# The weight load beside the index queries' rope: issued behind the eight row swaps instead of in front of them

## The reference

```python
    u = rms_norm(x, norm_g) * (1 + scale[:, None]) + shift[:, None]     # "the third norm"
    z = u @ w_in
    (aq, ak, av, ag, iq, ik, iw, bq, bk, bv, bg, cq, ck, cv, cg, ma, mb, mc) = jnp.split(z, SPLIT_OFFSETS, axis=-1)
    ...
    ya = dsa_attention(rope(aq), rope(ak), av, rope(iq), rope(ik), iw)   # iq, ik, iw choose the keys

def apply_rope(x, cos, sin):
    x1, x2 = jnp.split(x.astype(jnp.float32), 2, axis=-1)
    return jnp.concatenate([x1 * c - x2 * s, x1 * s + x2 * c], axis=-1).astype(x.dtype)
```

## Time and profile before

| | us |
|---|---|
| median of 3 runs | 2800.11 |
| the runs | 2791.91, 2800.11, 2801.91 |
| the profiled execution | 2794.37 |
| its span | 2792.6 |
| PE busy | 2681.3 (96%) |
| DVE busy | 1816.1 (65%) |
| ACT busy | 1152.6 (41%) |
| DMA from issue to landing, 1 MB weight load, median | 5.3 |
| DMA from issue to landing, 64 KB swap, median | 2.2 |

### The profile page before, as it was taken

The page is one execution under the profiler, slowest core; times in us unless marked ns, Lnnn a source line. Parts: engine busy times, 40 slices in busy tenths (PEclk is TensorE's granted clock), DMA queues, the critical chain, the costliest instruction groups (busy, mean ns, idle before and its releaser), DMA issues.

```text
span 2792.6 us, 36953 instructions
## 1 busy us (share of the span) xinstructions
PE 2681.3 (96%) x14886; PEld 2154.3 (77%) x14886; DVE 1816.1 (65%) x2968; ACT 1152.6 (41%) x1900; POOL 693.0 (25%) x514
## 2 busy tenths in 40 slices
PE   6999899999999998999999999998999999999997
PEld 5877578888878676888887878776787788777776
DVE  7789668867577775877557768744546548544534
ACT  3243544323242454433224464344434455444432
POOL 0000047988700004356540032000100122000100
PEclk9999999999999998999999999999999999999999
DMA  8453034554432112344432535231223222322312
GB/s 273 122 144 104 29 121 151 166 166 159 147 119 57 59 59 83 121 143 150 139 123 85 163 94 159 85 106 33 91 64 106 85 73 80 91 76 72 96 61 78
DMA packets 281114, 302.59 MB, mean 108 GB/s; under 512 B 9968, under 2 KB 263024, under 8 KB 280944
## 3 DMA queue, kind: packets, MB, share of 16 engines
q1 hardware_dynamic: 267568, 250.21, 28.8%
q0 software_dynamic: 13088, 49.55, 5.4%
q10 hardware_dynamic: 288, 0.47, 0.1%
HBM read 289.97 MB, written 2.10 MB: 105 GB/s over the span
## 4 chain that ended last, share of the span: by engine, by line
PE 86%; DVE 7%; ACT 4%; DMA 1%; issue 1%; SPq 0%; POOL 0%; DVEq 0%; ACTq 0%
PE ps L568 84%; PE ps L776 2%; DVE wl L1410 1%; DVE hl L1416 1%; DVE adaacc L1416 1%; DMA raw<-in_w_in 1%; ACT wh L934 0%; DVE recat L1708 0%; ACT recat L934 0%; ACT hh L934 0%; DMA stage<-in_w_ada 0%; DVE rawt L1416 0%; DMA t1s<-rawt 0%; ACT att_p L934 0%; DVE ca L1416 0%
## 5 line engine op out<-in xcount | busy, mean ns | idle before, releaser
L568 PE MATMUL ps<-hh,wh 128*128 128x512 f32 x2208 | 891.8, 404 | 24.1 <-DVE wl L1410 10.2
L568 PE MATMUL ps<-hh,wl 128*128 128x512 f32 x2208 | 866.8, 393 | 0.0
L568 PE MATMUL ps<-hl,wh 128*128 128x512 f32 x2208 | 865.5, 392 | 0.0
L1410 DVE TENSOR_TENSOR wl<-raw,wh 128x2048 fp32r<-128x2048 f32 (+3 forms) x234 | 500.9, 2149 | 167.7 <-ACT wh L934 167.5
L568 PEld LDWEIGHTS ps<-hh,wh 128*128 128x128 f32 x2208 | 416.5, 189 | 140.8 <-issue 40.4
L568 PEld LDWEIGHTS ps<-hh,wl 128*128 128x128 f32 x2208 | 416.4, 189 | 92.4
L568 PEld LDWEIGHTS ps<-hl,wh 128*128 128x128 f32 x2208 | 417.3, 189 | 80.2
L934 ACT ACTIVATE wh<-raw 128x2048 fp32r<-128x2048 f32 (+3 forms) x234 | 370.0, 1591 | 205.8 <-PE ps L568 191.4
L568 PE MATMUL ps<-fh,wh 128*128 128x512 f32 x432 | 171.6, 397 | 0.0
L568 PE MATMUL ps<-fh,wl 128*128 128x512 f32 x432 | 168.3, 390 | 0.0
L568 PE MATMUL ps<-fl,wh 128*128 128x512 f32 x432 | 168.2, 389 | 0.0
(11 more groups left out here) (298 smaller groups left out, 4136.5 us busy)
## 6 DMA issues: line engine op xcount, KB each, us to landing
raw<-in_w_in SPq DMA_DIRECT2D x75, 1024.0 KB, 5.3
raw<-in_w_up SPq DMA_DIRECT2D x46, 1024.0 KB, 5.1
strewn<-in_w_ada POOLq DMA_DIRECT2D x80, 512.0 KB, 4.1
raw<-in_w_ada SPq DMA_DIRECT2D x24, 1024.0 KB, 5.3
raw<-in_w_in SPq DMA_DIRECT2D x44, 512.0 KB, 5.1
raw<-in_w_out SPq DMA_DIRECT2D x16, 1024.0 KB, 5.1
raw<-in_w_down SPq DMA_DIRECT2D x16, 1024.0 KB, 5.2
stage<-in_w_ada SPq DMA_DIRECT2D x8, 1024.0 KB, 11.6
```

The lines of the kernel that those rows point to most:

```text
L568: return e.matmul(o, a, b, start=start, stop=stop, skip_group_check=True)
L1410: return e.tensor_tensor(o, a, b, op)
```

## The change

Of the splits in the list, the one that stands right in front of the unit `em` of a third norm (`split cq0`) no longer issues loads. The loads that it freed are issued at `rope iq1` instead, after its four swaps. All engines but SP have the same instructions in the same order.

```diff
-    for kind, *rest_ in X.order:
+    for n, (kind, *rest_) in enumerate(X.order):
         if kind == "rope":
             rope(*rest_[:3])
         elif kind in ("split", "ada", "adap"):
             free.add(rest_[-1])
+        if kind == "split" and X.order[n + 1][:1] == ("em",) and X.order[n + 1][1][0] == "m3":
+            continue
+        if kind in ("split", "ada", "adap") or kind == "rope" and rest_[1:3] == ["iq", 1]:
             while loads and loads[0][1]["raw_before"] in free:
                 load(*loads.pop(0))
```

## The result

| | before | changed |
|---|---|---|
| median | 2798.22 us, 20 runs | 2791.29 us, 20 runs |
| lowest and highest | 2787.97, 2806.32 | 2780.86, 2799.48 |
| the profiled execution's span | 2792.6 | 2795.5 |

The ratio is 0.9976, 95% interval 0.9966 to 0.9985: 6.7 us less, with an interval of 4.2 to 9.5. The forecast was 8.45 us less and 2791.7.

A forecast was written before the change was run, and what follows sets the result against it. PE, busy 96% of the span, was taken as the bound, leaving its idle time and low-clock stretches to gain. Layer 0's 4.3 us plus layer 1's 4.15 made 8.45 us (0.30%), from 2800.11 to 2791.7, range 2783 to 2800.

The forecast's parts named there:

- Landing with the load: Third norm, both layers: a swap issued behind the weight load waits for it; without it, landing was taken as 2.0 us.
- Layer 1, 4.15 forecast: PE sets the end: `cq1` starts 2.55 us earlier and regains 1.6 us of clock, together 4.15 us.
- The rival in which the clock does not come back: Layer 1, `cq1`: low clock stays, so the layer gives 2.55 us and the whole 6.9, 2793.2; chance 0.10.
- Layer 0, 4.3 forecast: DVE sets the end: its `wl` of `ck0` comes earlier and the gain goes on; 4.3 us taken.
- DVE's restart: Layer 0: DVE waits for `iq1` until 1523.6, then two steps of 0.7 us end at 1525.0 instead of 1529.63.
- the 4.6 of the undisturbed case: Layer 0: DVE's `rest iq1` ends 4.6 us earlier with 2.0 us landings, before other items cost some tenths.
- the 0.3 that I had: Layer 0: DVE loses 0.3 us beside POOL's `ik` product; if the row's 1.0 us returned whole, the layer gives 3.6.
- The late load: Layer 0: `ck0`'s load, now last, has cover of 0.3 us at 5.9 us landing, 1.0 us at the median landing.
- The slower rival: The late load decides: layer 0 loses from a landing of x = 10.8 us on; 15 us gives 2805; chance 0.04.
- The swaps slow of themselves: Both layers: eight swaps in a row stay slow and only start 1.07 us earlier; 2798.0, chance 0.05.
- More comes back: Layer 0: low-clock stretches behind both idle times go too, up to twice 1.6 us more; 2788.5, chance 0.05.
- The waits forecast for the profile: ACT waits for `iq0` 2.5 us (layer 0), 3.5 (layer 1), for `ck0`'s load some 5; PE idles 2 to 3 before `ck0`.

The follow-up runs named there:

- e3: Changed kernel with the load behind the four swaps of `iq0` only, ahead of those of `iq1`; ratio to before 0.9972, layer 0 distance 30.94 us.
- e6: Kernel before, old order, the moved load bringing only one eighth of its chunk; distances 30.03 us (layer 0) and 15.29 us (layer 1), no ratio.
- e5: Against the changed kernel, the load is issued at its old time from ACT's DMA queue, the swaps staying on SP's; ratio to before 0.9992.
- e1: Kernel before with the load moved behind the eight swaps in layer 0 only; ratio to before 0.9971, layer 0 distance 29.42 us.
- e11: Changed kernel with forty fulfilled waits on DVE at the start of the last feed-forward products; layer 0 distance 29.63 us, no ratio.
- e4: Changed kernel with the load behind all ten swaps, those of `ik` too; ratio to before 0.9963, layer 0 distance 30.56 us.
- e8: Changed kernel with forty fulfilled waits on SP ahead of the loads of the last feed-forward products; ratio to before 0.9965, layer 0 distance 29.18 us.
- e10: Changed kernel with forty fulfilled waits on PE behind the second tile of the last feed-forward products; layer 0 distance 28.96 us, no ratio.

## Why the prediction was right

*Forecast and sum.* The mechanism held at every step that carries it, and the sum of 8.45 us stands against 2.9 + 4.3 = 7.2 by the traces and 6.7 (4.2 to 9.5) by the runs. That the median of 2791.29 lies only 0.4 us from the forecast of 2791.7 is luck: the forecast started from a median of 3 runs, 2800.11, which 20 runs put 1.9 us lower, and the gain was forecast some 1.5 us too large. The two errors cancel. And 14 us, which I took as the least that can be told from no change, was too coarse: 20 runs of each kernel gave an interval of 4.2 to 9.5 us.

*Landing with the load* is shown by e3 (swaps behind the load are late, those ahead are not) and e6 (few bytes, swaps of 2.0 us in layer 1, and in layer 0 but for those beside the packet), and e5 adds what the rows before could not say, that the queue is not the reason.

*Layer 1, 4.15 forecast, 4.3 measured.* All eight swaps landed in 1.9 to 2.0 us, where 2.0 was taken, ACT's wait came out at 3.48 where 3.5 was forecast, and `cq1` starts with no idle time and runs at 1.00. The rival in which the clock does not come back had its chance in eight kernels that moved the load here behind the swaps of `iq0`; the distance was 15.1 and the granted clock over the tile 1.00 in each. The Trainium skill (TensorE: Matmul & The Clock Gate, Part 1) has the monitor's window run freely, by which rule this could change from run to run. The start of the kernel, 0.86 against 0.95 in the first 70 us, agrees with that; at this tile no trace showed it.

*Layer 0, 4.3 forecast, 3.6 in the profiled pair, 2.9 on average.* The term that was mis-sized is DVE's restart, which came later than summed up. I had `iq1` landed 7.15 us behind the mark and two steps of 0.7 us after it. DVE's timeline of the changed kernel:

```profile
1532.96 0.69 DVE L1410 TENSOR_TENSOR t1s<-t1s,cst 128x512 f32<-128x512 f32 x1 [4.39 <-DMA t1s<-rawt]
1533.69 0.69 DVE L1410 TENSOR_TENSOR iq<-iq,t1s 128x512 f32<-128x512 f32 x1
1535.00 1.17 DVE L1410 TENSOR_TENSOR t1s<-t1s,cst 128x512 f32<-128x512 f32 x1 [0.62 <-DMA t1s<-rawt]
1536.20 0.69 DVE L1410 TENSOR_TENSOR iq<-iq,t1s 128x512 f32<-128x512 f32 x1
...
1542.05 2.28 DVE L1410 TENSOR_TENSOR wl<-raw,wh 128x2048 fp32r<-128x2048 f32 x1
```

`iq1` was there at 7.76, 0.6 late: SP's chain has one swap that took 1.25 us to issue instead of 0.6 (1.88 in e1, where layer 0 came out 0.7 us worse). And its first step took 1.17 us, beside POOL's product of `ik`, 1.29 us from 1534.33 on. Together they take 1.1 us off the 4.6 of the undisturbed case, of which I had kept 4.3. The price was 0.5 us, not the 0.3 that I had nor the 1.0 of the row before. The Trainium skill (SBUF — State Buffer, "Who interferes with whom") has the instruction issued second wait until the first is over. By that rule DVE would wait until 1535.62 and end at 1536.31; the trace has 1536.17 and agrees within 0.14 us.

*The late load.* It landed in 6.4 us, not 5.9, `wh` was done at 1541.94, and DVE came to `wl` at 1542.05. The cover of 0.3 us that I gave it was 0.1, and in e11, where the load took 6.9 us, DVE waited 0.27 us for `wh`. The slower rival never came near: its x of 10.8 us stands against 6.4, and with the load 2.3 us later still, in e4, the layer keeps 1.8 us.

*The swaps slow of themselves* is out: the eight of layer 1 landed in 1.9 to 2.0 us. *More comes back* is out as well: layer 0 gave less than forecast, not more, and in the profiled pair nothing outside the two places moved.

*The waits forecast for the profile.* ACT's wait in layer 0 was to be 2.5 us and was 3.5 to 4.1, since the fourth swap landed in 3.2 us (3.8 in e1) and not in 2.0. It cost nothing in the profiled pair, as DVE waited for `iq1` anyway; in e1 it cost PE 0.53 us of idle time before `cq1`. ACT's wait for the load, 5.8 us where some 5 were forecast, came. PE's idle time, 2.4 us, came in the size forecast but not at the place: it stands before `iw` and ends with ACT's copy of `cq0`, behind the late split, and not before `ck0` with DVE's `wl`. I had given that copy room. It had none: `iw` ended at 1544.34 and `wl` at 1544.33, and `ck0` started at 1544.48.

## What to carry to other kernels

A small transfer whose result is waited for should start ahead of a large prefetch that has slack, on whatever queue either stands: behind or beside 1 MB it lands about when that does. How far back the large one may go is set by the first of its readers; count to that reader's neighbours in its engine's queue, and stop where the load has no cover left. Where runs differ by more than the effect, take short distances between marks inside the traces, and take each more than once.

## What the runs showed of the hardware

- Two DMA queues did not keep a 64 KB transfer out of the way of a 1 MB one: 4.1 to 6.5 us to landing in layer 0 and 3.8 to 5.3 in layer 1, instead of 2.0 (e5).
- Two executions of the same code lay 10.8 us apart at the first mark, and 7.3 of these came up in the first 200 us, with a granted clock of 0.86 against 0.95 in the first 70 us and 0.90 against 0.98 in the next.
- A 16 KB packet of kind instruction beside 64 KB transfers went with a landing of 3.2 to 3.8 us instead of 2.0 and a DMA issue on SP of 1.2 to 1.9 us instead of 0.6. Forty instructions more on PE moved the packet 1.2 us earlier, and the late landing and the slow issue to earlier swaps; forty on SP or DVE moved nothing (e8, e10, e11).
